# A two-layer hybrid decoder: a layer's two additions moved from VectorE to GpSimd, and empty expert slots left out of the indirect DMAs

## The reference

```python
def rglru_mixer(x, norm_w, w_in, conv_w, conv_b, w_rgate, b_rgate, w_igate, b_igate, lam, w_out):
    h = rmsnorm(x, norm_w)
    xb, gb = jnp.split(h @ w_in, 2, axis=-1)
    gate = jax.nn.gelu(gb, approximate=True)
    ...                                  # xc: causal convolution of xb over 4 taps
    r = jax.nn.sigmoid(... xr, w_rgate ...); i = jax.nn.sigmoid(... xr, w_igate ...)
    log_a = -LRU_C * r * jax.nn.softplus(-lam); a = jnp.exp(log_a)
    mult = jnp.sqrt(-jnp.expm1(2.0 * log_a))
    _, hs = lax.associative_scan(_lru_combine, (a, xc * i * mult), axis=1)
    return (hs * gate) @ w_out

def hier_moe(x, norm_w, w_group, w_expert, w_gate, w_up, w_down):
    h = rmsnorm(x, norm_w)
    ...                                  # each token: best group of 4, then 2 of its 8 experts
    def expert_block(args):              # a block of 128 rows of h and its expert e
        xblk, e = args
        return (jax.nn.silu(xblk @ w_gate[e]) * (xblk @ w_up[e])) @ w_down[e]
    ...                                  # rows times their weights, two per token added up

def reference(x, ...):
    for layer in range(2):
        x = x + (gla_mixer if layer == 0 else rglru_mixer)(x, ...)
        x = x + hier_moe(x, ...)
    return rmsnorm(x, final_norm)
```

## Time and profile before

| | us |
|---|---|
| median of 3 runs | 3018.33 |
| lowest and highest | 3016.26, 3020.65 |
| the profiled execution | 3014.33 |
| its span, first to last instruction | 3012.6 |

### The profile page before, as it was taken

One profiled execution on the slowest core, in us unless ns is written; L12 is line 12 of the kernel. 1 busy time (PEld: TensorE's weight loads), 2 busy tenths in 40 slices (PEclk: granted clock), 3 DMA queues, 4 the chain that ended last, 5 costly groups with the idle time before them and its releaser, 6 DMA issues. The chain is left out here.

```text
span 3012.6 us, 41660 instructions
## 1 busy us (share of the span) xinstructions
PE 2619.9 (87%) x12246; PEld 2100.4 (70%) x12246; DVE 1820.9 (60%) x3169; ACT 1647.7 (55%) x2260; POOL 590.5 (20%) x795
## 2 busy tenths in 40 slices
PE   6999999999799599999976999999599589999850
PEld 4878878788688477777755777777488467777640
DVE  4555555554456566565636888877465577556546
ACT  5565565554344366565635666675444376555532
POOL 0000000000011344555430000000011255545420
PEclk9999999999899799999987999999799799999985
DMA  3223223331445589789866545451444599877867
GB/s 122 90 91 101 89 91 105 104 107 57 142 155 167 173 295 312 273 281 323 271 218 215 175 166 168 144 171 63 128 154 147 178 350 337 289 264 265 307 237 293
DMA packets 388258, 573.61 MB, mean 190 GB/s; under 512 B 33408, under 2 KB 304000, under 8 KB 384000
## 3 DMA queue, kind: packets, MB, share of 16 engines
q1 hardware_dynamic: 353104, 457.23, 45.8%
q0 software_dynamic: 32688, 105.99, 9.4%
q10 hardware_dynamic: 2304, 8.39, 0.7%
HBM read 449.32 MB, written 122.22 MB: 190 GB/s over the span
## 5 line engine op out<-in xcount | busy, mean ns | idle before, releaser
L1445 DVE TENSOR_TENSOR experts_gu_lo<-carry_raw,experts_gu_hi 128x1024 fp32r<-128x1024 f32 x256 | 296.6, 1220 | 64.4 <-ACT experts_gu_hi L1404 62.4
L1327 POOL DMA_INDIRECT experts_rows<-h_rows,experts_source_now x194 | 269.8, 1391 | 274.0 <-PE experts_ps L1497 129.3
L118 PE MATMUL experts_ps<-experts_gu_hi,experts_hT_hi 128*128 128x512 f32 x760 | 316.3, 416 | 3.0 <-issue 3.0
L119 PE MATMUL experts_ps<-experts_gu_lo,experts_hT_hi 128*128 128x512 f32 x760 | 300.3, 395 | 0.0
L120 PE MATMUL experts_ps<-experts_gu_hi,experts_hT_lo 128*128 128x512 f32 x760 | 299.9, 395 | 0.0
L1404 ACT ACTIVATE experts_gu_hi<-carry_raw 128x1024 fp32r<-128x1024 f32 x256 | 250.2, 1057 | 52.5 <-DMA carry_raw<-in_moe_w_up 42.8
L1456 DVE TENSOR_TENSOR experts_hT_lo<-experts_ps,experts_hT_hi 128x512 fp32r<-128x512 f32 x194 | 133.2, 687 | 240.6 <-ACT experts_hT_hi L1383 233.6
L963 POOL MEMSET route_empty<- 128x512 int32 x2 | 1.1, 564 | 1322.1 <-POOLq L160 1322.1
L118 PE MATMUL route_ps<-route_w_hi,route_src_hi 128*128 128x512 f32 x512 | 208.6, 407 | 45.7 <-DVE route_src_lo L1029 45.7
L1396 ACT ACTIVATE experts_y<-experts_ps,experts_by_block 128x1024 f32<-128x1024 f32 x99 | 110.6, 1117 | 213.8 <-DMA y_rows<-experts_y,experts_target_now 208.4
L119 PE MATMUL route_ps<-route_w_lo,route_src_hi 128*128 128x512 f32 x512 | 203.4, 397 | 0.0
(11 more groups left out here) (322 smaller groups left out, 6757.1 us busy)
## 6 DMA issues: line engine op xcount, KB each, us to landing
carry_raw<-in_moe_w_gate SPq DMA_DIRECT2D x64, 1024.0 KB
carry_raw<-in_moe_w_up SPq DMA_DIRECT2D x64, 1024.0 KB
ahead_wd_raw<-in_moe_w_down SPq DMA_DIRECT2D x64, 1024.0 KB
gla_w_raw<-in_gla_w_in SPq DMA_DIRECT2D x32, 1024.0 KB, 7.3
ahead_wd_raw<-in_lru_w_in SPq DMA_DIRECT2D x32, 1024.0 KB
gla_w_raw<-in_gla_w_in SPq DMA_DIRECT2D x32, 512.0 KB, 5.1
route_src<-oT_rows SPq DMA_DIRECT2D x32, 512.0 KB
x_rows<-route_x_new SPq DMA_DIRECT2D x32, 512.0 KB, 2.9
```

What stands on the lines that cost most here:

```text
L118: nc.tensor.matmul(out, w_hi, x_hi, start=first, stop=False)
L119: nc.tensor.matmul(out, w_hi, x_lo, start=False, stop=False)
L1327: pool.indirect_dma_start(rows[:, b], None, h_halves[b], bass.IndirectOffsetOnAxis(source_now[b][:].bitcast(U32), 0))\
L1445: nc.vector.tensor_tensor(gu_lo[:, slot(e), of_part(c)], gu_raw[:, slot(e), of_part(c)], gu_hi[:, slot(e), of_part(c)].bitcast(F32), ALU.s ...
```

## The change

Two edits. In `lru` `combine` is taken from DVE's list, and a list for POOL is added that does the same two additions for all 16 tiles one after another, with the same waits and the same increments of `x_done`. It doesn't stand between other instructions there: a tile is added as soon as its x and y are in. In `experts` the words of `sources` are no longer masked, so that an empty slot names row 2048 or above, and the gathers have a bound of T - 1; the stores have a bound of 2T - 1. A row outside its bound is not transferred. `rows` is set to zero once at the start of the stage, since slots that are skipped keep what was there.

```diff
@@ experts, gpsimd @@
             pool.memset(y[:], 0.0)
+            pool.memset(rows[:], 0.0)
             pool.memset(aT_hi[:].bitcast(F32), 0.0)
...
                 pool.indirect_dma_start(rows[:, b], None, h_halves[b],
-                                        bass.IndirectOffsetOnAxis(source_now[b][:].bitcast(U32), 0))\
+                                        bass.IndirectOffsetOnAxis(source_now[b][:].bitcast(U32), 0),
+                                        bounds_check=T - 1, oob_is_err=False)\
                     .then_inc(rows_in[b], DMA)
...
                 pool.indirect_dma_start(y_rows, bass.IndirectOffsetOnAxis(target_now[:].bitcast(U32), 0),
-                                        y[:], None).then_inc(y_stored, DMA)
+                                        y[:], None, bounds_check=2 * T - 1, oob_is_err=False).then_inc(y_stored, DMA)
@@ experts, vector @@
-                nc.vector.tensor_scalar(sources[:, columns], lists[:, columns, 0], 1, T - 1,
-                                        ALU.logical_shift_right, ALU.bitwise_and).then_inc(sources_set, 1)
+                nc.vector.tensor_scalar(sources[:, columns], lists[:, columns, 0], 1, None,
+                                        ALU.logical_shift_right).then_inc(sources_set, 1)
@@ lru, vector @@
-            def combine(t):
-                j = t % 2
-                after_dma(dve, x_in[j], t // 2)
-                after_dma(dve, y_in[j], t // 2)
-                step(nc.vector.tensor_tensor(x[:, j], x[:, j], y_ab[:, j, 0], ALU.add))
-                nc.vector.tensor_tensor(x[:, j], x[:, j], y_ab[:, j, 1], ALU.add).then_inc(x_done, 1)
...
-            combine(0)
             normalise(0)
             for t in range(GT):
-                combine(t + 1)
                 take_hT(t, 2 * (t % 2))
...
                 gated_input(n)
-                if t + 1 < NT:
-                    combine(t + 1)
                 ratio(n)
@@ lru, gpsimd @@
+        @block.gpsimd
+        def _(pool):
+            step = Steps(pool, pool_order)
+            for t in range(NT):
+                j = t % 2
+                after_dma(pool, x_in[j], t // 2)
+                after_dma(pool, y_in[j], t // 2)
+                step(pool.tensor_tensor(x[:, j], x[:, j], y_ab[:, j, 0], ALU.add))
+                pool.tensor_tensor(x[:, j], x[:, j], y_ab[:, j, 1], ALU.add).then_inc(x_done, 1)
```

More of the change, by code:

```diff
@@ L1683, in lru @@
         y_stored = m.plain("y_stored")
-        order = m.plain("vector_order")
+        order, pool_order = m.plain("vector_order"), m.plain("pool_order")
         block = m.block()
```

## The result

The changed kernel takes 3060.11 us (median of 4 runs, 3053.44 to 3063.31), the kernel before 3017.83 (3016.26 to 3020.65) beside it. The ratio is 1.0136, with a 95% interval from 1.0117 to 1.0155: 42 us slower. The forecast was 3026, 8 us slower, and the range ended at 3056. The size was not right; the direction was, but 8 us were the small rest of two large terms, and only one of the two came. The profiled execution is the fastest of the four, 3053.44 us.

A forecast was written before the change was run, and what follows sets the result against it. Experts bound by DMA in one stretch, otherwise by PE with gaps; the recurrent layer by a DVE-ACT-PE ring. Profiled 3014.3 + 40 (layer) - 32 (skipped slots) = 3022.3, against the median 3026 us; range 2980 to 3056.

The forecast's parts named there:

- The additions leave DVE: Recurrent steps: removing DVE's two 1.22 us additions per tile gains 0, since DVE then waits for ACT's decays anyway.
- The additions arrive on POOL, and hold DVE: Recurrent layer: POOL's 2.1 us additions and DVE's two-input work block each other, 4.1 us a step; +40 us, 15 to 58.
- the sign that the prediction gave: Profile after, recurrent layer: additions on POOL with a mean of 2.1 us, between 0.94 and 2.83.
- The start of the layer: Recurrent layer up to the first step: uncovered first addition and h meeting POOL's additions, +3 us, bounds -1 and +8.
- Skipped slots: Both expert stages: untransferred empty slots shorten PE's waits for rows, -32 us in sum, gain between 12 and 65.
- the price of the comparison: Expert stages: the bound's added work in POOL's three indirect issues a block, taken at 0 as POOL idles part of each block.
- waits in front of near-empty blocks: Layer 0's experts: seven PE waits for blocks with few rows, 10.2 of 25.5 us; 10 us taken as gain.
- the stretch at 98% of the DMA engines: Layer 1's experts, 2414 to 2592: bound by DMA; 6.3 MB of empty slots are 18 us, 17 taken as gain.
- Rival 1: Recurrent layer, DVE between scans and y: no hold, 2986 us, chance 0.18; held by one addition of two, 3006, chance 0.12.
- Rival 2: Expert stages: the comparison lengthens POOL's issues, 0.11 us each undoes the gain, 3058 us; chance 0.10 together with Rival 3.
- Rival 3: Expert stages: a skipped slot keeps its place and time in the queue, gain 0, 3058 us; chance 0.10 with Rival 2.
- one of those of being wrong: Signs against the forecast: steps keep 31.4 us, queue's bytes or PE's waits stay, or waits for full blocks go too.

The follow-up runs named there:

- b5: Kernel before, but from tile 5 on GpSimd adds, first beside VectorE's PSUM reads, then after its gated input; tiles 0 to 4 on VectorE: 3015.77 us, ratio 0.9999.
- a1: Kernel before with only the additions moved to GpSimd, indirect DMAs unchanged: 3062.64 us, ratio 1.0150.
- b2: Kernel before plus two GpSimd additions per tile into a buffer nothing reads, VectorE's additions kept: 3054.33 us, ratio 1.0127.
- b3: Kernel before plus five GpSimd memsets per tile into a buffer nothing reads, VectorE's additions kept: 3017.28 us, ratio 1.0002.
- a2: Kernel before with only the skipped slots, bounds on gathers and stores, additions left on VectorE: 3010.26 us, ratio 0.9982.
- a3: Kernel before with bounds on gathers and stores, set so that no slot is skipped: 3023.59 us, ratio 1.0022.
- d2: Kernel before with bounds on the gathers alone, set so that no slot is skipped: 3021.58 us, ratio 1.0019.
- a4: Kernel before with gathers that skip every row but token 0's, leaving the experts' input out; stores as before: 3013.31 us, ratio 0.9995.
- a5: Kernel before, loading only half the weight rows of experts 2 to 31, the rest left out: 2962.87 us, ratio 0.9825.
- d1: a5 with skipping bounds on both gathers and stores: 2945.06 us, ratio 0.9759 to the kernel before, against a5's 2962.87 us.
- d4: Kernel before with skipping bounds on stores alone (3005.18 us), plus the second gather's list copied ahead of the store: 3007.72 us, ratio 0.9971.

## Why the prediction came out as it did

**The additions leave DVE: 0.** Right. b5 has 22 of them fewer on DVE and the time of before.

**The additions arrive on POOL, and hold DVE: +40 (15 to 58).** Right in mechanism and size, and in place for six of nine steps: +42.6 us in after's trace, +45 in a1. Undisturbed an addition takes 2.34 us, where 2.1 was taken between 0.94 and 2.83; beside DVE 2.4 to 3.4, so that the mean of all 32 is 2.85 us, just above the sign that the prediction gave. The estimate of 2.25 us from the Trainium skill, GPSIMD Engine Reference, section Elementwise — side-by-side cycle accounting, was the nearer one, and its 3 us more would have brought the layer to +43. The start of the layer was put at +3 and is +4.4. The evidence in before was one-sided (POOL held by DVE); that the hold is mutual was a choice, and b2 and b3 show it: additions on POOL do it, writes alone don't. That the total came so near is in part luck: additions 0.24 us longer than taken and three steps that went another way nearly cancel.

**Skipped slots: -32.** This is the step that failed, the price of the skipped bytes in PE's waits: a2 measured -5.4, and no bound of it (12 to 65 us of gain) held it. It had two mistakes.
One is the price of the comparison, taken at 0. It is 6.6 us (a3), and the gathers' alone cost 5.7 (d2).
The larger one is what the bytes are worth: 12 us at most (a2 against a3) and not 32. For layer 0 I counted ten us for waits in front of near-empty blocks, as if such a wait were the time of the block's bytes. Of the ten 1.6 us went: after the change PE still waits 8.7 us in seven such places. The median gather of such a block took 6.3 us to land and its bytes are some 1.2 of these; before the change the minimum was 3.4 us, and 2.2 is left with none. The same row had said it: a gather of a full block, issued beside 3 MB of weights, reached PE after 8.9 us. For the stretch at 98% of the DMA engines I took all bytes saved at the stretch's rate, 17 us of PE's 19.7 idle. The bytes went (16.80 to 10.11 MB), the share went from 0.98 to 0.90, and PE gained 2.8 us, which the next stretch lost again. A busy share of the engines says how long they work, and not that PE's idle time is proportional to it: PE waits for single gathers, and these take 6.2 us even without bytes (a4), beside weights that have the same size as before. Loading half the weights moved this (a5), and only then skipping was worth 18 us and more (d1). What the rest of a gather's 6 us is, and why skipping wins more in d1, stays open.

**Rival 1** (no hold, or by one addition of two) is refuted by a1's 45 us and b2's 38. **Rival 2** (longer issues): its mechanism is there, 0.13 us a gather, and it costs 7 us, not 32, since most issues are hidden (argued; no run shows which); that was argued rightly, but only as a reason to price it at nothing. **Rival 3** (a skipped slot keeps its place and its time: 3058) names the time that came out, 3060, for half the reason: the place in the queue stays, 32688 packets before and after, and the packet's time goes from 159 to 9 ns. With rival 2 it had a chance of 0.10 together, too little: what spoke against it, that "the engines' time goes with bytes", is true of the engines, and says nothing on PE.

**The range** ended at 3056, 2 us below the two rivals. A single term of -32 whose lower bound was 12 could only have been bounded by 0, since the prediction showed no row in which a gather with fewer bytes lands earlier. Of its signs the bytes came (6.7 MB gone in the stretch, some 6 forecast), and one of those of being wrong was met: PE's waits stayed. With 0 in its place the forecast's own terms give 3018.3 + 40 = 3058, and the result lies well inside what the layer's bounds leave around it.

## What to carry to other kernels

Before pricing saved bytes, look at one transfer: how long from issue to landing, and how much of that its own bytes are; if its bytes are 1 us of 6, fewer of them win little, however busy the DMA engines are. Here less of the other traffic helped; another order of issues was tried once (d4) and didn't. A bound on an indirect DMA costs a little in every issue, so measure it apart for each kind: here stores, for which PE doesn't wait directly, win 10 us alone, and gathers lose 5. Work with inputs in SBUF that is moved to GpSimd is not free for VectorE: place it where VectorE idles or reads PSUM, or leave it; and moving work off an engine that isn't late at that place wins nothing.

## What the runs showed of the hardware

- GpSimd's addition of 128 x 1024 fp32 takes 2.34 us, VectorE's 1.22. While both engines work with two inputs from SBUF each waits for the other (after): GpSimd up to 3.4 us, VectorE's scan of 1.27 up to 3.44, its h of 1.28 up to 2.88, and a subtraction of 2.28 up to 4.48.
- GpSimd's memset (0.95 us) holds nothing on VectorE, in 80 of them. Its multiplication by a constant, with one input, takes 2.76 us at the shortest and 3.08 in the median, longer than the addition in the same place (1.89 and 2.42), and holds VectorE for less in all: +10 against +38 us.
- In nine steps of after the 128 x 2 copy behind the scans takes 2.1 us in place of 0.17, and y behind it its usual 1.21. Whether the copy, with one input, is held itself or the wait of y is booked on it, the rows don't tell.
- GpSimd's issue of an indirect DMA waits for VectorE too: in the first expert stage of before it takes 1.00 us with VectorE idle (median of 48), 0.99 beside a VectorE instruction with an input in PSUM (47), and 1.57, at most 2.45, when it starts under one with both inputs in SBUF (58).
- Rows that an indirect DMA skips leave their packet, of 4 or 8 bytes, with 9 ns of an engine; all packets stay. A gather of 128 rows of 2 KB lands 3.4 us after its issue at best, with no row to bring 2.2 us.
- A bound on a gather adds a register move of 29 ns ahead of the issue, starts it 0.07 us later and makes it some 0.06 us longer.
